# A hybrid-attention encoder with 32 gated experts on one core: the first block's rows picked by products, three-word pair records, and adjacent gate and up columns

## What is computed

```python
h = rmsnorm(x, ffn_norm)                      # 768 x 1024
g = argmax(h @ router_group + bias)           # 1 of 4 groups
e = top2(h @ router_expert + bias, in group)  # 2 of the 8 experts of the group
for e in range(32):                           # each token counts for its 2 experts
    y = (silu(h @ w_gate[e]) * (h @ w_up[e])) @ w_down[e]   # 1024 -> 256 -> 1024
    out += gates[:, e] * y
y = rmsnorm(x + out, final_norm)
```

## Time and profile before

| | |
|---|---|
| median of 3 runs | 810.87 us (810.26 to 811.95) |
| the profiled execution: its own time | 810.43 us |
| the profiled execution: first to last instruction (span) | 808.6 us |
| TensorE busy (page, part 1) | 717.3 us, 89% |
| VectorE, ScalarE, GpSimd busy | 322.4, 214.0, 201.0 us |
| gate and up products L1670, 1280 records | 156.8 us busy, mean 396 ns |
| down products L1679, 320 records | 80.6 us busy |
| transposes of rows L1660 | 29.1 us busy, idle before them 15.7 us |
| transposes of the hidden rows L1709, 40 | mean 328 ns |
| moved by DMA | 154.64 MB |

### The profile page before, as it was taken

One profiled execution on the slowest core, in us unless ns is written; L12 is line 12 of the kernel. 1 busy time (PEld: TensorE's weight loads), 2 busy tenths in 40 slices (PEclk: granted clock), 3 DMA queues, 4 the chain that ended last, 5 costly groups with the idle time before them and its releaser, 6 DMA issues. The chain is left out here.

```text
span 808.6 us, 12300 instructions
## 1 busy us (share of the span) xinstructions
PE 717.3 (89%) x3978; PEld 401.0 (50%) x3979; DVE 322.4 (40%) x900; ACT 214.0 (26%) x575; POOL 201.0 (25%) x478
## 2 busy tenths in 40 slices
PE   6899999999978999999999974999997999999910
PEld 3455544444455666664555552555553555555500
DVE  3853121100088988881545562111121112112138
ACT  2433210011177766761211110111110111111122
POOL 1224232220024230232001223442332334442110
PEclk9999999999999999999999986999998999999975
DMA  8702002000050000000792158799999999999856
GB/s 297 301 1 105 0 1 103 2 0 1 18 196 1 1 1 1 1 2 0 326 422 86 79 215 313 262 353 368 374 348 390 383 340 372 404 375 384 346 222 257
DMA packets 36728, 154.64 MB, mean 191 GB/s; under 512 B 9642, under 2 KB 10794, under 8 KB 23744
## 3 DMA queue, kind: packets, MB, share of 16 engines
q1 hardware_dynamic: 29024, 138.20, 45.0%
q0 software_dynamic: 7648, 15.75, 5.9%
HBM read 142.29 MB, written 20.03 MB: 201 GB/s over the span
## 5 line engine op out<-in xcount | busy, mean ns | idle before, releaser
L1405 PE MATMUL banks<-arena 128*128 128x512 f32 (+1 forms) x384 | 163.8, 580 | 9.5 <-DMA arena<-w_in 7.7
L1670 PE MATMUL banks<-arena 128*64 128x256 f32 x1280 | 156.8, 396 | 4.7 <-issue 2.2
L1670 PEld LDWEIGHTS banks<-arena 128*64 128x64 f32 x1280 | 93.7, 137 | 60.6 <-issue 10.9
L1405 PEld LDWEIGHTS banks<-arena 128*128 128x128 f32 x384 | 72.3, 193 | 85.1 <-issue 77.8
L1561 PE MATMUL banks<-arena 128*128 128x512 f32 x192 | 86.4, 598 | 1.1 <-DVE arena L1162 1.1
L1679 PE MATMUL banks<-arena 128*64 128x512 f32 x320 | 80.6, 615 | 0.5 <-ACT arena L980 0.5
L1326 DVE TENSOR_TENSOR arena<-arena,banks 128x128 f32<-128x128 f32 x40 | 11.5, 288 | 164.6 <-ACT arena L972 164.6
L1118 DVE TENSOR_REDUCE arena<-banks 128x1 f32<-128x512 f32 (+1 forms) x96 | 55.3, 599 | 48.5 <-PE banks L1477 41.5
L903 ACT ACTIVATE arena<-banks,arena 128x512 f32<-128x512 f32 (+1 forms) x96 | 58.2, 611 | 42.7 <-DVE arena L1121 20.5
L1561 PEld LDWEIGHTS banks<-arena 128*128 128x128 f32 x192 | 35.1, 190 | 38.8 <-issue 37.5
L972 ACT ACTIVATE arena<-banks 128x128 f32<-128x128 f32 x40 | 11.1, 277 | 161.9 <-PE banks L1670 161.9
(11 more groups left out here) (179 smaller groups left out, 852.8 us busy)
## 6 DMA issues: line engine op xcount, KB each, us to landing
arena<-w_gate SPq DMA_DIRECT2D x32, 1024.0 KB, 12.6
arena<-w_up SPq DMA_DIRECT2D x32, 1024.0 KB, 13.2
arena<-w_down SPq DMA_DIRECT2D x32, 1024.0 KB, 13.4
arena<-w_in SPq DMA_DIRECT2D x3, 2048.0 KB, 8.3
arena<-pair_rows SPq DMA_DIRECT2D x5, 1024.0 KB, 11.2
arena<-w_out SPq DMA_DIRECT2D x1, 4096.0 KB, 12.8
arena<-xT SPq DMA_DIRECT2D x6, 512.0 KB, 10.4
arena<-x SPq DMA_DIRECT2D x6, 512.0 KB, 10.8
```

The lines of the kernel that those rows point to most:

```text
L1405: last = nc.tensor.matmul(bank(mm % 2)[:, 0:GROUP_COLS[g]], xgT[:, t, c, :], w[:, c, :], start=(c == 0), stop=(c == DC - 1))
L1670: last = nc.tensor.matmul(bank(b)[h * SLOTS:(h + 1) * SLOTS, 0:2 * P].rearrange("p (g n) -> p g n", g=2), x_eT[i][:, c, :], w[:, :, c, h, ...
```

## The change

1. **First block of expert 0 by products.** For each tile VectorE makes `select`, the one-hot of the slot times mask of expert 0 times the token's norm (`choose`), and TensorE multiplies it with `x_tok` into bank 4; ScalarE copies the sum to `x_sel`, and 16 products with quarters of the identity transpose it. The gather of expert 0 is gone.
2. **The gain moves.** `h2` is now x times the norm only, on ScalarE; ffn_norm's gain is multiplied in when the transposed rows leave PSUM (a copy becomes a product with a broadcast operand), from a new small load `gain_rows`.
3. **Pair records of three words** (token, result row of either half): no arithmetic on the ids that are read back. That load goes to ScalarE's queue, after the first silu, and SyncE no longer waits for the scatters; expert 31's load waits for the row products (`chosen_psum`). The store of the last residual tile goes ahead of the loads of experts 4 and 5.
4. **Gate and up read adjacent columns**; the hidden rows are then put in order by four 64x64 products with the identity in place of one transpose, behind an `await_count`.
5. **Order on TensorE.** `place` of the last tile goes ahead of the counts; in the first group the counts are awaited after the first gate and up; `down` of expert 0 runs before `gate_up` of expert 1.

```diff
-    ids_dram = nc.dram_tensor("pair_of_slot", (T * NE, 1), u32).ap()
+    ids_dram = nc.dram_tensor("pair_of_slot", (T * NE, 3), u32).ap()
...
@@ sync
-            sp.dma_start(gain_ffn, A["ffn_norm"].to_broadcast([P, D])).then_inc(gffn_in, 16)
...
+            store_residual(NT - 1)
             load_expert(0, 4)
             load_expert(0, 5)
-            store_residual(NT - 1)
-            sp.wait_ge(ids_scattered, 2 * NT * 16)
-            for h in range(2):
-                sp.dma_start(yids_sb[h * SLOTS:(h + 1) * SLOTS, NE:].rearrange("r (b e) -> r b e", e=NE),
-                             ids_dram.rearrange("(b r e) o -> r b (e o)", b=NBLK, e=NE)[:, 1:, :]).then_inc(ids_loaded, 16)
             sp.wait_ge(x2_stored, NT * 16)
...
+            sp.wait_ge(chosen_psum, 1)
             load_expert(NGRP - 1, members(NGRP - 1)[-1])
@@ gpsimd
                     with pool.If(n > 0):
+                        await_count(ids_loaded, 32)
                         await_count(e_xeT_psum, before + 1)
...
-            gather_main(0, 0)
+            pool.sem_inc(id_ready, 1)
             gather_main(0, 1)
...
-            pool.wait_ge(ids_ready, 3)
+            pool.wait_ge(ids_ready, 2)
@@ scalar
+            def ffn_norm(t):
+                act.wait_ge(norm_ready, t + 1)
+                if t >= 2:
+                    act.wait_ge(h2_stored[t % 2], 16 * (t // 2))
+                act.activation(h2[t % 2].rearrange("n (c p) -> n c p", c=DC), x_tok[:, t, :].rearrange("n (p c) -> n c p", c=DC),
+                               ACT.Copy, scale=rs[:, t:t + 1]).then_inc(h2_ready, 1)
...
+                ffn_norm(t)
+            act.wait_ge(chosen_psum, 1)
+            act.activation(x_sel, bank(4), ACT.Copy).then_inc(chosen_rows, 1)
             act.wait_ge(gates_in, 1)
...
                     silu(e + before)
+                    if isinstance(g, int) and e == 0:
+                        load_further_ids()
@@ vector
+            def choose(t):
+                for i, mask in enumerate((m1_all, m2_all)):
+                    dve.tensor_scalar(share[:, i:i + 1], mask[:, t, 0:1], rs[:, t:t + 1], None, ALU.mult).then_inc(dve_chain, 1)
+                    chain[0] += 1
+                dve.wait_ge(dve_chain, chain[0])
+                dve.wait_ge(onehot_ready, 2 * t + 2)
+                link(dve.tensor_scalar(select[:, t, :], onehot[:, 0, 0:SLOTS], share[:, 0:1], None, ALU.mult))
+                dve.scalar_tensor_tensor(select[:, t, :], onehot[:, 1, 0:SLOTS], share[:, 1:2], select[:, t, :],
+                                         ALU.mult, ALU.add).then_inc(select_ready, 1)
...
             slots(NT - 1)
+            dve.wait_ge(xeT_psum, 1)
+            dve.tensor_tensor(x_eT[0], bank(0).rearrange("p (c n) -> p c n", c=DC), gain_eT, ALU.mult).then_inc(xeT_ready, 1)
 
             dve.wait_ge(counts_psum, 1)
...
-                        dve.tensor_copy(x_eT[(s + 1) % 2], bank(0).rearrange("p (c n) -> p c n", c=DC)).then_inc(xeT_ready, 1)
+                        dve.tensor_tensor(x_eT[(s + 1) % 2], bank(0).rearrange("p (c n) -> p c n", c=DC), gain_eT, ALU.mult).then_inc(xeT_ready, 1)
@@ tensor
+            def choose(t):
+                pe.wait_ge(select_ready, t + 1)
+                for h in range(2):
+                    last = nc.tensor.matmul(bank(4)[h * SLOTS:(h + 1) * SLOTS, :], select[:, t, :],
+                                            x_tok[:, t, h * 512:(h + 1) * 512], start=(t == 0), stop=(t == NT - 1))
+                return last
...
+            for t in range(3):
+                choose(t)
             rank(NT - 1)
-            counts = bank(1)[:, 0:NE]
+            choose(3)
+            place(NT - 1)
+            choose(4)
+            choose(5).then_inc(chosen_psum, 1)
+            counts = bank(2)[:, 0:NE]
...
-            place(NT - 1)
...
-                w = w[:, 0:4096].rearrange("p (g c n h) -> p g c h n", g=2, c=DC, h=2)
+                w = w[:, 0:4096].rearrange("p (g c n) -> p g c n", g=2, c=DC)
...
-                                                x_eT[i][:, c, :], w[:, :, c, h, :],
+                                                x_eT[i][:, c, :], w[:, :, c, h * P:(h + 1) * P],
...
-                pe.wait_ge(h_ready, k + 1)
-                nc.tensor.transpose(bank(3)[:, 0:P], h_tok, ident).then_inc(hT_psum, 1)
+                await_count(h_ready, k + 1)
+                h_row = h_tok.rearrange("n (m j) -> n j m", j=2)
+                for j in range(2):
+                    for h in range(2):
+                        half = slice(h * SLOTS, (h + 1) * SLOTS)
+                        last = nc.tensor.matmul(bank(3)[half, j * SLOTS:(j + 1) * SLOTS], h_row[half, j, :], ident[half, half],
+                                                start=True, stop=True)
+                last.then_inc(hT_psum, 1)
...
+                    if early:
+                        down_weights(g, 0)
+                        down_before(k, g, 0, last_done)
...
-            pe.wait_ge(rows_in[0], 16)
-            rows_transpose(0, 0, range(DC)).then_inc(xeT_psum, 1)
-            pe.wait_ge(counts_ready, 1)
+            pe.wait_ge(chosen_rows, 1)
+            x_sel_c = x_sel.rearrange("n (p c) -> n c p", c=DC)
+            for c in range(DC):
+                for h in range(2):
+                    half = slice(h * SLOTS, (h + 1) * SLOTS)
+                    last = nc.tensor.matmul(bank(0)[half, c * SLOTS:(c + 1) * SLOTS], x_sel_c[half, c, :], ident[half, half],
+                                            start=True, stop=True)
+            last.then_inc(xeT_psum, 1)
```

More of the change, by code:

```diff
@@ L275, in build @@
         macc = m.take(NT * NE).rearrange("p (t e) -> p t e", t=NT)
-        bias_r = m.take(NG + NE)
-        ones = m.take(P)
-        logit = m.take(NT * (NG + NE)).rearrange("p (t e) -> p t e", t=NT)
-        top = m.take(1)
-        max_g, max_1, max_2 = (m.take(NT) for _ in range(3))
-        rank_f = m.take(2)
-        onehot = m.take(2 * P).rearrange("p (i n) -> p i n", i=2)
-        slot_of = m.take(4 * NE).rearrange("p (i w e) -> p i w e", i=2, w=2)
         r_g = m.take(3 * NG)
@@ L286, in build @@
         slot_f = m.take(2)
-        junk_c = m.take(256).bitcast(bf16)
+        rank_f = m.take(2)
+        bias_r = m.take(NG + NE)
+        top = m.take(1)
+        max_g, max_1, max_2 = (m.take(NT) for _ in range(3))
+        share = m.take(2)
+        assert m.at <= WORDS - 3 * NBLK * NE
+        m = Area(WORDS - 3 * (NBLK - 1) * NE, WORDS - DC * (NG + NE) - DC)
         cnt = m.take(NE)
@@ L291, in build @@
         pk = m.take(NGRP * RING)
+        logit = m.take(NT * (NG + NE)).rearrange("p (t e) -> p t e", t=NT)
         m = Area(WORDS - DC * (NG + NE) - DC, WORDS)
@@ L304, in build @@
         x_eT = [m.take(DC * SLOTS).rearrange("p (c n) -> p c n", c=DC) for _ in range(3)]
-        silu_t = m.take(P)
-        h_tok = m.take(P)
-        h_T = m.take(P)
+        assert m.at <= WORDS - 3 * NBLK * NE
+        dead = CONST["upper"][0]
+        assert CONST["rev_g"][0] - dead >= 3 * P
+        silu_t, h_tok, h_T = (const_sb[:, dead + i * P:dead + (i + 1) * P] for i in range(3))
         m = Area(W0 + SLOT_W, QKV0)
@@ L497, in _ @@
                     sp.dma_start(gain_cols, A["ffn_cols"]).then_inc(lam_loaded, 16)
+                    sp.dma_start(gain_rows, A["ffn_norm"].rearrange("o (p c) -> (o p) c", c=DC)).then_inc(lam_loaded, 16)
                     for i, n in enumerate(("diff_lq1", "diff_lk1", "diff_lq2", "diff_lk2")):
@@ L711, in await_count, with gather @@
                 pool.sem_inc(waited, 1)
-            def gather(i, ids, column, ready, count):
-                pool.tensor_copy(id_cur[0:SLOTS, i:i + 1], ids[0:SLOTS, bass.ds(column, 1)]).then_inc(ready, 1)
+            def gather(i, column, ready, count):
+                pool.tensor_copy(id_cur[0:SLOTS, i:i + 1], ids_sb[0:SLOTS, bass.ds(3 * column, 1)]).then_inc(ready, 1)
                 await_count(ready, count)
@@ L721, in scatter @@
             def scatter(i, column, ready, count):
-                pool.tensor_copy(yid_cur[:, i:i + 1], yids_sb[:, bass.ds(column, 1)]).then_inc(ready, 1)
+                pool.tensor_copy(yid_cur[:, i:i + 1], ids_sb[:, bass.ds(3 * column + 1, 1)]).then_inc(ready, 1)
                 await_count(ready, count)
@@ L1261, in _ @@
                 x2T_evac(t)
-                ffn_norm(t)
+                norm(t)
                 route(t)
@@ L1716, in pe_group @@
             def pe_group(g):
-                words = load_counts(pe, g)
+                first = isinstance(g, int) and g == 0
+                if not first:
+                    words = load_counts(pe, g)
                 for s in members(g):
                     e = g * RING + s
-                    n, before = extras(words, s)
-                    k = e + before
                     if is_last(g, s):
@@ L1726, in pe_group @@
                         pe.wait_ge(up_loaded[s], 16 * (g + 1))
+                    early = first and s == 1
+                    if not first or s:
```

(12 more changed lines are left out.)

85 lines of the change are left out of this document (42 added, 43 removed).

## The result

The changed kernel takes 829.43 us (median of 4 runs, 827.34 to 829.65), the kernel before 810.87: the record's ratio is 1.0204, 95% interval 1.0182 to 1.0225 (the quotient of the two medians is 1.023). Slower by about 2%, where 0.5% faster was forecast. The profiled execution has a span of 827.9 us against 808.6, so 19.3 us are to be found.

The account below looks back on a forecast made before the run. TensorE was taken to set the pace until about 680 us, with weights level at the end. Start -6.0 us plus loop +2.3 gives -3.7, so 807.2 us on the median of 810.87; range 801.5 to 815.

Parts of the forecast that it names:

- the five rivals: Outcomes: as summed 0.38, adjacent columns gain nothing 0.24, quarters unpaired 0.09, smaller start gain 0.11, larger gain 0.18.
- The start: Hole near 480 us: expert 0's gate and up 8.4 us earlier, expert 2's 6.0 us earlier.
- the rows of expert 1: At the start: gather issue to rows 7.6 us, rows there at 493.9, gate and up of expert 1 at 498.9.
- The ordinary block: Expert loop: gate and up -0.18 us, hidden rows +0.14, so -0.04 per block; 25 blocks give -1.0 us.
- Rivals B: Gate and up: the gapped read is not what lengthens records; 7.0 us more, 814.2 us; chance 0.24.
- C: Hidden rows: the quarter products don't pair; 0.24 us more in 30 blocks, 7.3 us, 814.5 us; chance 0.09.
- Further blocks and group starts: Expert loop: +0.25 us each without issued work in stock; 8 further blocks +2.0 us, 5 group starts +1.3 us.
- A shift before 680 us arrives at the end: Whole loop: shifting TensorE's work before about 680 us shifts the weights too, so the start's 6.0 us gain isn't held back.
- The front at nothing, within 0.5 us: Under projections and attention: small load, wider zero fill and pair records cost nothing; 0.5 us either side if uncovered.
- The chance for "slower": Whole kernel slower by more than 1.6 us: 0.31, from dearer products, no paired quarters or a smaller start gain.

Follow-up runs that it names:

- b_poolpad: The kernel before with eight more waits in each of six hardly taken branches of GpSimd's looped group: 820.73 us, ratio 1.0104.
- a_light: The changed kernel loading only a quarter of each weight matrix for experts 6 to 30, same instructions, other results: 800.69 us, ratio 0.9856.
- b_light: The kernel before loading only a quarter of each weight matrix for experts 6 to 30, other results: 803.68 us, ratio 0.9906.
- b_p4: The kernel before with only adjacent columns and the four quarter products put in: 811.08 us, ratio 1.0004.
- a_p4undone_flat: The changed kernel with every second column and one hidden-row transpose per block again, and GpSimd's groups written out: 815.55 us, ratio 1.0044.
- b_flat: The kernel before with GpSimd's loop over the groups written out: 816.02 us, ratio 1.0047.
- a_front: The changed kernel with its two small loads moved from the start to behind the output projection's weight load at 222 us: 827.70 us, ratio 1.0167.
- a_pe128: The changed kernel with 128 semaphore increments at the head of TensorE's program: 831.06 us, ratio 1.0256.
- b_late128: The kernel before with 128 waits on an already raised semaphore in TensorE's program ahead of its wait for expert 0's rows: 812.45 us, ratio 1.0005.
- a_late64: The changed kernel with 64 waits on an already raised semaphore in TensorE's program just ahead of expert 0's chosen rows: 823.55 us, ratio 1.0137.

## Why the prediction was wrong

The forecast was 807.2 us (801.5 to 815.0), faster with 0.54; measured 829.43.

- **A cost that was not in the sum: instructions.** Every step priced what instructions do and none that they have to be fetched. TensorE's holes, with the lower clock behind one of them, are 13.1 us of the 19.3 us, GpSimd's 6.9. The view that could have warned was there: the DMA part of the page lists q8 and q14 as "instruction", DMA is full in the loop, and the group start's 0.61 us of issue is the turn of TensorE's own loop. The Trainium skill, "Runtime: NRT & Kernel Launch" (section "Instruction fetch mechanics"), says that crossing a 16 KiB block is "mostly hidden" and that a taken branch out of the loaded window stalls. The trace agrees on the packets' 16 KB at TensorE's holes and, through b_poolpad and the packets behind GpSimd's branch, with a stall at a jump back; it disagrees on the first where DMA is full, with holes of up to 3.4 us (3.03 of it idle in the row at 558.53). None of the five rivals held this, and the range ended at 815.
- **The start: right in kind, too large.** Expert 0 at -8.8 us (8.4 forecast), routing 1.1 us earlier (1.0). The term that failed is the rows of expert 1. ScalarE's norm takes 2.15 us, about the bound named and not the 1.06 taken, so the last store of h2 leaves as late as before (482.62 less 4.9, against 477.6) and the first gather at 492.77 - 4.9 = 487.9, where 486.3 was taken; the rows come 7.9 us behind it (7.6 taken), at 500.64 - 4.9 = 495.7 instead of 493.9. TensorE waits 2.85 us for them and pays half clock after it (down in 3.14 us, not 1.94). Expert 2: -4.1 us in the profile, -2.0 in a_light against b_light (each from its own front), instead of -6.0.
- **The ordinary block: right.** -0.04 to -0.05 us against -0.04: the record's median is 379 ns against 387 (0.13 to 0.17 us per block, 0.18 forecast), and the quarters pair: 0.38 us from their first to the next gate and up, against 0.26.

```profile
517.03 3.67 PE L1670 MATMUL banks<-arena 128*64 128x256 f32 x32
520.63 0.71 PE L1660 MATMUL banks<-arena 64*128 64x64 f32 x8
521.27 1.94 PE L1679 MATMUL banks<-arena 128*64 128x512 f32 x8
523.14 0.46 PE L1713 MATMUL banks<-arena 64*64 64x64 f32 x8
523.52 3.67 PE L1670 MATMUL banks<-arena 128*64 128x256 f32 x32
```

  (b_p4, in the form of the earlier trace rows.) Rivals B and C are refuted by it. The step of two words does cost 8 ns of 387 (387 in the kernel before, 379 in b_p4), against the Trainium skill's note that I had weighed, by which such a step is free ("SBUF — State Buffer", "Door 1: The DMA port swizzle").
- **Further blocks and group starts: too dear.** +3.3 us was taken for them; a_light less b_light falls by 1.5 us from expert 2 to the last, 0.04 per block over all of them, so they cost about nothing more.
- **"A shift before 680 us arrives at the end": wrong.** The wait of L531 for products (19.4 us) showed slack at 640 us, and I read it as TensorE setting the pace to the end. The 0.60 us at expert 30 was the better sign: it means no reserve, and b_p4 and a_p4undone_flat lose all their lead there. In the changed kernel the same wait is 30.4 us, because TensorE is late; in a_p4undone_flat, where it is early, 7.6.
- **The front at nothing, within 0.5 us.** It is +4.9 in the profile, from clock falls that come without the change too (b_flat); the error is in the width, since one profile was taken as what each execution does.

The chance for "slower" stood at 0.31, for a loss of 3 to 4 us by dearer products; what came is 20 us at two places where none was looked for, so where that chance points the right way, it is luck.

## What to carry to other kernels

In a kernel whose DMA engines are full, count the instructions that a change adds, above all to a looped body, and look for "issue" idle time beside the instruction packets; hardly executed branches cost 9 us here by their length. Before believing in a gain at the start, look at the last wait on the other stream: where it is longer than zero, the gain ends there. To see what an edit does by itself, compare both kernels with the traffic thinned out.

## What was not expected of the hardware

- TensorE stopped for up to 3.4 us inside a run of products at a 16 KB instruction packet while the DMA share was 1.02 (3.7 in a_front), and not at 0.55 with the same program. It went on 1.3 to 1.6 us after the packet's end each time.
- 48 waits more in GpSimd's loop: 2.87 to 9.17 us at its turn. The packets of q14 are 8 KB and mostly take 0.3 to 0.5 us each. Three lie in the changed kernel's 6.30 us behind the branch, and the last ends 1.24 us before GpSimd goes on; what fills the 3.3 us ahead of the first is open, as is why at full traffic only some placements of TensorE's code run dry.
- Semaphore increments on TensorE's queue followed each other at 0.15 us (a_pe128). 128 waits on a raised semaphore took 6.8 us (b_late128, from 484.27 us on), 53 ns each; where products were still running, as in a_late64, only part of that was idle time.
- The granted clock fell to its lower level after idle times of 1.2 to 3.2 us in the profiles of b_flat and the changed kernel, and stayed at 1.00 after idle times of 1.2 to 2.1 us at the same places of the kernel before.
